# A dilated attention group in eight steps of two heads by four token tiles, with one copy-out place

## The chip, the cores and the metric

The kernel runs on one core of a Trainium2 chip. The metric is the time of one execution on the device, in microseconds (us). The engines are named as in the profile: PE is TensorE (PEld its weight loads), DVE is VectorE, ACT is ScalarE, POOL is GpSimd, SP is SyncE, which here only issues DMAs.

## The reference, cut to what matters

Two transformer blocks run one after the other over 1024 tokens of width 1024. The second block has, beside a latent attention, a dilated attention of 24 heads of width 64, in three groups of eight heads. The groups see keys at distances that are multiples of 1, 4 and 16, within a window:

```python
DIL_CONFIGS = ((128, 1), (512, 4), (2048, 16))
for g, (window, dilation) in enumerate(DIL_CONFIGS):
    o, lse = dilated_group(q[:, :, sl], k[:, :, sl], v[:, :, sl], dilation, window // (2 * dilation))
alpha = jax.nn.softmax(jnp.stack(lses, axis=0), axis=0)
out = jnp.sum(alpha[..., None] * outs, axis=0)
```

In `dilated_group` the scores of a query against its keys are masked, the maximum is subtracted, and out come exp, the sum `den`, and the weighted sum of the values. In the third group (dilation 16) the kernel puts the tokens of two residues into a tile of 128, so a tile of queries needs exactly one tile of 128 keys. In the first two groups it needs two (up to 256 keys).

## The kernel before

The dilated stage projects k, v and q of each group from the normalized input and runs the attention steps in the gaps. The work is written out by hand in slots. `D_UNITS` has 72 units (3 groups, then k, v, q, then 8 pieces each). Unit u is projected by PE in slots 2u and 2u + 1, in twelve matmuls of 512 columns each (`d_proj`, L1203). Slots 144 to 151 hold four units of the gates instead (units 16 to 19 of `gate_part`, L1118). After slot 151 comes the end of a phase, where PE, ACT and DVE wait for each other, and the gates go on with unit 20.

Each k or q unit is roped by DVE in slot 2u + 2: `rope_cos` (one instruction, L2279) and `rope_sin` (four instructions of 32 partitions, L2289, and an addition, L2295), which raises `roped`.

A step of attention takes one pair of heads (j) and some tiles of tokens. `step_at` says in which slot it begins. In that slot PE makes the scores (`d_scores`, L1219, into banks 3 and 4), DVE adds the mask and takes the maximum (`d_soft`, L2309), ACT takes the exponentials (`d_exp`, L1745). In the next slot PE transposes the result (`d_transposes`, L1232) and ACT copies it out of the accumulator (`d_pT`, L1754). In the slot after that PE multiplies by the values (`d_values`, L1251, bank 7), DVE copies the result into `osb` (`d_out`, L2318), and SP stores it (`d_store`, L628).

What decides about waits is the order within a slot, for each engine its own:

- PE: scores of a step that begins here, then twelve matmuls of the projection, then the values of the step two slots back, then the transposes of the step one slot back. Only the first two steps of a group have their scores behind the projection.
- DVE: `rope_cos`, `d_soft`, `d_out`, `rope_sin`. Only in the slot of a group's first step does `rope_sin` come before `d_soft`.
- ACT: `d_exp`, then `d_pT`.

The third group has 16 steps of two heads by two tiles, one in each of the slots 134 to 149. One step has 4 score matmuls of 128 columns, 4 of the mask and maximum, 4 exponentials, 4 transposes, 4 value matmuls, one copy of 512 and one of 256 elements, and 2 stores. A float32 matmul shows in the trace as two passes, so four of them are "x8". `osb` has two places of 256 elements, used in turn. The scores of a step wait for `d_max` of the step before, and the first of the steps of a head pair for `roped` of the pair's second q unit.

Of the kernel before, what the change touches and what calls it, by code (L numbers as in the profile page):

```python
# [98 lines left out]
def hybrid_blocks_kernel(nc, x, w_in, pool_w, pool_scale, attn_sinks, w_out, norm_pre, norm_post,  # L99
# [390 lines left out]
    def d_step(g, i):  # L490
        return 4 * 4 * g + i

    def step_of(g, i):

        j, r = divmod(i, 4)
        if g == 0:
            tiles = 2 * r, 2 * r + 1
        elif g == 1:
            tiles = 4 * (r % 2) + r // 2, 4 * (r % 2) + 2 + r // 2
        else:  # L500
            tiles = 2 * r, 2 * r + 1
        return j, tiles

    STEP_LAG = 4
    step_at = {}
    for u_, (g_, kind_, t_) in enumerate(D_UNITS):
        if kind_ == "q" and (g_ < 2 or t_ % 2):
            n_steps_ = 2 if g_ < 2 else 4
            for i_ in range(n_steps_):
                step_at[2 * u_ + STEP_LAG + i_] = g_, (2 * t_ if g_ < 2 else 4 * (t_ // 2)) + i_  # L510
    D_GATES = 4
# [13 lines left out]
    def gate_bank(u):  # L525

        return {47: 7, 19: 6, 20: 5}.get(u, u % 4)

# [42 lines left out]
    def _(sp):  # L571
# [51 lines left out]
        def d_store(g, i):  # L623
            n = d_step(g, i)
            j, tiles = step_of(g, i)
            sp.wait_ge(*after("d_out", n + 1))
            for b, t in enumerate(tiles):
                sp.dma_start(d_rows(g, t)[:, P * j:P * j + P].rearrange("p (a d) -> p a d", a=2),  # L628
                             osb[:, n % 2, 2 * b:2 * b + 2, :]).then_inc(sem(f"d_store{n % 2}"), 16)

        def stats_store(g):

            sp.wait_ge(*after("d_exp", G * d_step(g, 16)))
# [175 lines left out]
    def _(pe):  # L809
# [397 lines left out]
        def d_scores(g, i):  # L1207
            n = d_step(g, i)
            j, tiles = step_of(g, i)
            if i % (4 if g == 2 else 2) == 0:  # L1210
                q_unit = i // 2 if g < 2 else i // 2 + 1
                pe.wait_ge(*after("roped", 16 * g + 8 + q_unit + 1))
            if n >= 1:
                pe.wait_ge(*after("d_max", n))
            for b, t in enumerate(tiles):
                k0, nk, _, _ = window(g, t)
                for a in range(2):
                    rows = slice(HD * a, HD * a + HD)
                    m = pe.matmul(ps[:, 3 + a, 256 * b:256 * b + nk], qTd[rows, j % 2, P * t:P * t + P],  # L1219
                                  kTd[rows, j, k0:k0 + nk], start=True, stop=True)  # L1220
            m.then_inc(sem("d_scored"), 1)

        def d_transposes(g, i):
            n = d_step(g, i)
            pe.wait_ge(*after("d_exp", G * (n + 1)))
            if n >= 1:
                pe.wait_ge(*after("d_pT", n))
            c = 0
            for b, t in enumerate(step_of(g, i)[1]):
                for a in range(2):  # L1230
                    for c0, width, _, _, _ in window(g, t)[3]:
                        m = pe.transpose(ps[:, 5 + c // 4, (c % 4) * P:(c % 4) * P + P],  # L1232
                                         prd[n % 2][:, 2 * b + a, c0:c0 + width], ident[:])
                        c += 1
            m.then_inc(sem("d_T"), 1)
# [20 lines left out]
        for slot in range(D_SLOTS):  # L1256
# [3 lines left out]
            if slot < 2 * N_D:  # L1260
                d_proj(slot)
            else:
                u, part = divmod(slot - 2 * N_D, 2)
                if part == 0 and u < 3:
                    pe.wait_ge(*after("d_read", N_D - 2 + u))
                elif part == 0:
                    pe.wait_ge(*after("d_pT", 2 * 16))
                gate_part(16 + u, part)
# [8 lines left out]

        pe.wait_ge(*after("d_max", 2 * 3 * TT))
        pe.wait_ge(*after("d_pT", 2 * 3 * TT))

# [93 lines left out]
        for j in range(n_t + 5):  # L1374
            if j < n_t:
                m_scores(j)
            if j == 0:
                pe.wait_ge(*after("d_out", 2 * 3 * TT))
                gate_unit(47)
# [23 lines left out]
    def _(act):  # L1403
# [331 lines left out]
        def d_exp(g, i):  # L1735
# [5 lines left out]
            for b, t in enumerate(tiles):  # L1741
                nk = window(g, t)[1]
                for a in range(2):
                    h, o, p_ = 2 * j + a, dstat[:, g % 2, t, :], prd[n % 2][:, 2 * b + a, 0:nk]
                    act.activation(p_, p_, ACT.Exp, scale=-1.0, bias=o[:, h:h + 1], accum_out=o[:, H1 + h:H1 + h + 1]).then_inc(sem("d_exp"), 1)  # L1745

        def d_pT(g, i):
            n = d_step(g, i)
            act.wait_ge(*after("d_T", n + 1))
            if n >= 1:  # L1750
                act.wait_ge(*after("d_valued", n))
            nb = G if g == 2 else 2 * G
            src = ps[:, 5:7, :].rearrange("p b (j c) -> p (b j) c", c=P)
            act.activation(pTd[:, 0:nb, :], src[:, 0:nb, :], ACT.Copy).then_inc(sem("d_pT"), 1)  # L1754

        for slot in range(D_SLOTS):
# [12 lines left out]
            if slot == D_SLOTS - 2:  # L1769
                act.wait_ge(*after("d_scored", 2 * 3 * TT))  # L1770
                act.wait_ge(*after("stats_out", 48))
# [18 lines left out]
        act.wait_ge(*after("roped", 6 * TT))  # L1790
        act.wait_ge(*after("d_valued", 2 * 3 * TT))
        gate_evac(range(16, 16 + D_GATES), gt2)
# [160 lines left out]
    def _(dve):  # L1953
# [317 lines left out]
        def rope_cos(u, r, g, kind, t):  # L2271
# [4 lines left out]
            if kind == "q" and (g or j >= 2):  # L2276
                dve.wait_ge(*after("d_scored", d_step(g, 4 * (j - 2) + 4)))
            dve.wait_ge(*after("d_done", u + 1))
# [18 lines left out]
        def d_soft(g, i):  # L2297
# [7 lines left out]
            for b, t in enumerate(tiles):  # L2305
                nk, mc = window(g, t)[1:3]
                for a in range(2):
                    h = 2 * j + a
                    last = nc.vector.tensor_tensor_reduce(prd[n % 2][:, 2 * b + a, 0:nk], ps[:, 3 + a, 256 * b:256 * b + nk], masks[:, mc:mc + nk],  # L2309
                                                          -1.0, BIG, ALU.add, ALU.min, accum_out=dstat[:, g % 2, t, h:h + 1])  # L2310
            last.then_inc(sem("d_max"), 1)

        def d_out(g, i):
            n = d_step(g, i)
            dve.wait_ge(*after("d_valued", n + 1))
            if n >= 2:
                dve.wait_ge(*after(f"d_store{n % 2}", 32 * (n // 2)))
            nc.vector.tensor_copy(osb[:, n % 2].rearrange("p b d -> p (b d)"), ps[:, 7, 0:256]).then_inc(sem("d_out"), 1)  # L2318

        for slot in range(D_SLOTS):  # L2320
# [15 lines left out]
            if slot == D_SLOTS - 2:  # L2336
                group_stats = [stats[:, 0], stats[:, 1], dstat[:, 0]]
                nm = [x_[:, :, 0:H1] for x_ in group_stats]
                den = [x_[:, :, H1:] for x_ in group_stats]
                dve.wait_ge(*after("d_scored", 2 * 3 * TT))  # L2340
                dve.wait_ge(*after("d_exp", G * 2 * 3 * TT))
                dve.wait_ge(*after("stats_in", 32))
# [133 lines left out]
```

## Time and profile before

| | us |
|---|---|
| median of 3 timed runs | 1712.38 |
| the three | 1711.75, 1712.38, 1715.34 |
| profiled execution, its own time | 1715.64 |
| span of its trace | 1713.8 |
| PE busy | 1681.7 (98%) |
| DVE busy | 831.0 (48%) |
| ACT busy | 560.6 (33%) |

The own time lies 1.8 us above the span. A busy PE is a modelled figure, since its matmuls overlap; starts of instructions are the better measure.

### The profile page before, as it was taken

How to read it: one execution, taken by the hardware profiler on the slowest of the kernel's cores; microseconds unless marked ns; L12 is line 12 of the kernel's file. 1: busy time of each engine (PE TensorE's matmuls, PEld its weight loads, DVE VectorE, ACT ScalarE, POOL GpSimd, SP SyncE). 2: the span in 40 equal slices, each digit the busy share in tenths (PEclk: the TensorE clock that was granted, in tenths of full speed). 3: DMA queues.
4: the chain of work that ended last, by engine and by line, in shares of the span. 5: the costliest groups of instructions: out<-in, count | busy, mean ns of one | idle time of the engine just before them, and what ended most of it. 6: DMA issues, size and time to landing. Idle time of an engine off the chain costs nothing.

```text
span 1713.8 us, 22561 instructions
## 1 busy us (share of the span) xinstructions
PE 1681.7 (98%) x8729; PEld 1390.4 (81%) x8729; DVE 831.0 (48%) x1630; ACT 560.6 (33%) x1288; POOL 510.3 (30%) x400
## 2 busy tenths in 40 slices
PE   7999999999999999999999999999999999999998
PEld 6778778889878787888878887787787999988886
DVE  4430245344343614558076653645521888855724
ACT  5101456324333003440034200441113777741211
POOL 6124033023333333022211133015313745534310
PEclk9999999999999999999999999999999999999999
DMA  6113012233257232111320223117465635226322
GB/s 205 50 68 105 13 62 70 87 119 93 74 208 270 87 117 81 32 44 51 115 75 21 70 74 111 32 50 266 127 230 160 144 64 139 53 68 212 109 113 98
DMA packets 97130, 178.44 MB, mean 104 GB/s; under 512 B 13912, under 2 KB 33792, under 8 KB 96896
## 3 DMA queue, kind: packets, MB, share of 16 engines
q1 hardware_dynamic: 61120, 95.57, 19.2%
q10 hardware_dynamic: 35904, 81.44, 13.5%
q8 instruction: 69, 1.13, 0.3%
q14 instruction: 37, 0.30, 0.1%
HBM read 122.05 MB, written 54.92 MB: 103 GB/s over the span
## 4 chain that ended last, share of the span: by engine, by line
PE 92%; DVE 4%; issue 1%; DMA 1%; POOL 1%; ACT 1%; ACTq 0%; DVEq 0%; POOLq 0%
PE ps L1203 22%; PE ps L1118 14%; PE ps L824 13%; PE ps L1056 5%; PE ps L1370 5%; PE ps L1310 5%; PE ps L958 4%; PE ps L1251 4%; PE ps L1340 4%; PE ps L1323 3%; PE ps L879 3%; PE ps L1219 2%; PE ps L1232 2%; PE ps L1010 2%; DVE rope_swapped L2289 1%
## 5 line engine op out<-in xcount | busy, mean ns | idle before, releaser
L711 POOL TENSOR_SCALAR w_hi<-w_stage 128x1024 fp32r<-128x1024 f32 (+3 forms) x140 | 127.4, 917 | 995.8 <-PE ps L1203 366.8
L718 POOL TENSOR_TENSOR w_lo<-w_stage,w_hi 128x1024 fp32r<-128x1024 f32 (+3 forms) x140 | 271.8, 1949 | 8.9
L1203 PE MATMUL ps<-h2T_hi,w_hi 128*128 128x512 f32 x384 | 157.0, 409 | 0.7 <-ACT gate_tiles L1618 0.7
L1118 PE MATMUL ps<-h2T_hi,w_hi 128*128 128x512 f32 x384 | 153.4, 400 | 0.5 <-issue 0.3
L1203 PE MATMUL ps<-h2T_hi,w_lo 128*128 128x512 f32 x384 | 153.0, 398 | 0.0
L1118 PE MATMUL ps<-h2T_lo,w_hi 128*128 128x512 f32 x384 | 152.3, 397 | 0.0
L1203 PE MATMUL ps<-h2T_lo,w_hi 128*128 128x512 f32 x384 | 151.9, 396 | 0.0
L1118 PE MATMUL ps<-h2T_hi,w_lo 128*128 128x512 f32 x384 | 151.3, 394 | 0.0
L1745 ACT ACTIVATE probs_dil<-probs_dil,dil_stats_out 128x256 f32<-128x256 f32 (+2 forms) x192 | 87.6, 457 | 155.9 <-DVE dil_stats_out L2309 155.3
L2289 DVE SCALAR_TENSOR_TENSOR rope_swapped<-ps,sin_table_T 32x512 f32<-32x512 f32 x192 | 132.0, 687 | 3.5
L2404 DVE TENSOR_REDUCE small<-ps 128x1 f32<-128x1024 f32 x64 | 77.7, 1214 | 55.1 <-PE ps L1310 54.9
L1310 PE MATMUL ps<-k_mla,q_mla 128*128 128x512 f32 x384 | 104.0, 406 | 0.0
L743 POOL TENSOR_SCALAR p_mla<-p_mla,small 128x1024 f32<-128x1024 f32 x64 | 71.7, 1120 | 87.3 <-DVE small L2397 87.1
L1203 PEld LDWEIGHTS ps<-h2T_hi,w_hi 128*128 128x128 f32 x384 | 72.6, 189 | 27.0 <-issue 9.4
L1766 ACT ACTIVATE values_out<-ps 128x512 f32<-128x512 f32 x24 | 14.4, 598 | 231.2 <-PE ps L1203 231.2
L2279 DVE SCALAR_TENSOR_TENSOR qT_dil<-ps,cos_table_T 128x512 f32<-128x512 f32 x24 | 23.2, 965 | 137.3 <-PE ps L1203 137.3
L2391 DVE TENSOR_TENSOR pT_mla_lo<-ps,pT_mla_hi 128x512 fp32r<-128x512 f32 x128 | 81.9, 680 | 14.0 <-ACT pT_mla_hi L1853 14.0
L1118 PEld LDWEIGHTS ps<-h2T_hi,w_hi 128*128 128x128 f32 x384 | 72.1, 188 | 18.8 <-POOL w_lo L718 0.7
L1853 ACT ACTIVATE pT_mla_hi<-ps 128x512 fp32r<-128x512 f32 x128 | 69.7, 596 | 52.3 <-PE ps L1323 52.3
L1203 PEld LDWEIGHTS ps<-h2T_hi,w_lo 128*128 128x128 f32 x384 | 72.6, 189 | 17.5
L1118 PEld LDWEIGHTS ps<-h2T_hi,w_lo 128*128 128x128 f32 x384 | 72.1, 188 | 17.3
L1203 PEld LDWEIGHTS ps<-h2T_lo,w_hi 128*128 128x128 f32 x384 | 72.7, 189 | 16.2
(294 smaller groups left out, 3751.8 us busy)
## 6 DMA issues: line engine op xcount, KB each, us to landing
w_stage<-in_w_in SPq DMA_DIRECT2D x76, 512.0 KB, 3.9
w_stage<-in_w_out SPq DMA_DIRECT2D x16, 512.0 KB, 3.8
gate_scr<-gate_tiles ACTq DMA_DIRECT2D x16, 512.0 KB, 3.8
gates<-gate_scr ACTq DMA_DIRECT2D x32, 256.0 KB, 3.3
v_dil<-v_dil_scr SPq DMA_DIRECT2D x25, 256.0 KB, 3.3
v_dil_scr<-values_out SPq DMA_DIRECT2D x24, 256.0 KB, 2.0
dil_scr<-dil_out SPq DMA_DIRECT2D x96, 64.0 KB, 1.6
dil_nums<-dil_scr ACTq DMA_DIRECT2D x24, 256.0 KB, 4.1
```

Of the source, the lines that this page charges most:

```text
L711: last = nc.gpsimd.tensor_scalar(hi_, raw_, 1.0, 0.0, ALU.mult, ALU.add)
L718: last = nc.gpsimd.tensor_tensor(lo_, raw_, hi_.bitcast(F32), ALU.subtract)
L824: m = pe.matmul(acc, a, b, start=(i == 0 and j == 0), stop=(i == len(pairs) - 1 and j == 2))
L1056: m = pe.matmul(ps[:, Y_BANKS[t % 4] + half, :], a[:, k, tk], b[:, s, k, :], start=(k == 0 and j == 0), stop=(k == KT - 1 and j == 2))
L1118: m = pe.matmul(ps[:, gate_bank(u), :], a[:, s, k, P * m_:P * m_ + P], b[:, k, COLS * n:COLS * n + COLS], start=(k == 0 and j == 0), stop= ...
L1203: m = pe.matmul(bank, a, b, start=(k == 0 and i == 0), stop=(k == KT - 1 and i == 2))
L1310: m = pe.matmul(ps[:, 2 * (i % 2) + n, :], Q[:, a, q], K[:, b, COLS * n:COLS * n + COLS], start=(j == 0), stop=(j == 2))
L1370: m = pe.matmul(ps[:, u % 8, :], a, b, start=(k == 0 and j == 0), stop=(k == 3 and j == 2))
L1745: act.activation(p_, p_, ACT.Exp, scale=-1.0, bias=o[:, h:h + 1], accum_out=o[:, H1 + h:H1 + h + 1]).then_inc(sem("d_exp"), 1)
L2289: last = nc.vector.scalar_tensor_tensor(rot[out_rows, 0, :], ps[rows, d_bank(u), :], -HD ** -0.5 if kind == "q" else -1.0, sinT[rows, COLS ...
L2391: nc.vector.tensor_tensor(PTl[dst], ps[:, 4 + half, :].rearrange("p (j c) -> p j c", c=P), PTh[dst].bitcast(F32), ALU.subtract).then_inc(s ...
L2404: nc.vector.tensor_reduce(rstd[:, j % 8:j % 8 + 1], ps[:, 2 * (j % 2):2 * (j % 2) + 2, :].rearrange("p b c -> p (b c)"), AX_X, ALU.max, ne ...
```

## The change

The third group runs in 8 steps of two heads by four tiles. They begin in every other slot (134, 136, ..., 148). Each has 8 of all that a step had 4 of, one copy of 1024 elements and one of 512, and 4 stores. The scores take the places of 128 columns in banks 3 and 4, the transposes both banks 5 and 6. `osb` is one place for this group, so a copy-out waits for all the stores of the step before. Gate unit 19 goes from bank 6 to bank 3 and waits for the last `d_max`. The counts of steps and exponentials follow. The numbers of matmuls, masks, exponentials and stores over the whole group stay. With i < 2 the steps 0 and 1 still have their scores behind the projection; step 1 now begins in slot 136.

```diff
     def step_of(g, i):
+        if g == 2:
+            j, r = divmod(i, 2)
+            return j, tuple(range(4 * r, 4 * r + 4))
         j, r = divmod(i, 4)
...
+    def exps_of(n):
+        return G * n + G * max(n - 32, 0)
+    def place(g):
+        return P if g == 2 else 2 * P
+    def probs_of(g, n):
+        return prd[n % 2].rearrange("p j (x k) -> p (j x) k", k=place(g))
...
-            n_steps_ = 2 if g_ < 2 else 4
-            for i_ in range(n_steps_):
-                step_at[2 * u_ + STEP_LAG + i_] = g_, (2 * t_ if g_ < 2 else 4 * (t_ // 2)) + i_
+            for i_ in range(2):
+                step_at[2 * u_ + STEP_LAG + i_ * (1 if g_ < 2 else 2)] = g_, (2 * t_ if g_ < 2 else 2 * (t_ // 2)) + i_
...
-        return {47: 7, 19: 6, 20: 5}.get(u, u % 4)
+        return {47: 7, 20: 5}.get(u, u % 4)
...
-            if i % (4 if g == 2 else 2) == 0:
-                q_unit = i // 2 if g < 2 else i // 2 + 1
+            if i % 2 == 0:
+                q_unit = i // 2 if g < 2 else i + 1
                 pe.wait_ge(*after("roped", 16 * g + 8 + q_unit + 1))
...
-            pe.wait_ge(*after("d_exp", G * (n + 1)))
+            pe.wait_ge(*after("d_exp", exps_of(n + 1)))
...
-                    pe.wait_ge(*after("d_pT", 2 * 16))
+                    pe.wait_ge(*after("d_max", D_STEPS))
...
-            nb = G if g == 2 else 2 * G
-            src = ps[:, 5:7, :].rearrange("p b (j c) -> p (b j) c", c=P)
-            act.activation(pTd[:, 0:nb, :], src[:, 0:nb, :], ACT.Copy).then_inc(sem("d_pT"), 1)
+            act.activation(pTd[:], ps[:, 5:7, :].rearrange("p b (j c) -> p (b j) c", c=P), ACT.Copy).then_inc(sem("d_pT"), 1)
...
             dve.wait_ge(*after("d_valued", n + 1))
-            if n >= 2:
-                dve.wait_ge(*after(f"d_store{n % 2}", 32 * (n // 2)))
-            nc.vector.tensor_copy(osb[:, n % 2].rearrange("p b d -> p (b d)"), ps[:, 7, 0:256]).then_inc(sem("d_out"), 1)
+            for b in range(n % 2, n % 2 + 1) if g < 2 else range(2):
+                m = (n + 1 - b) // 2
+                if m:
+                    dve.wait_ge(*after(f"d_store{b}", 32 * m + 32 * max(m - 16, 0)))
+            dst = osb[:, n % 2].rearrange("p b d -> p (b d)") if g < 2 else osb[:].rearrange("p x b d -> p (x b d)")
+            nc.vector.tensor_copy(dst, ps[:, 7, 0:256 if g < 2 else 512]).then_inc(sem("d_out"), 1)
```

## Rows read from the trace of the kernel before

**Rows 1.** The page, part 1: busy time of each engine, share of the span.

```profile
PE 1681.7 (98%) x8729; PEld 1390.4 (81%) x8729; DVE 831.0 (48%) x1630; ACT 560.6 (33%) x1288; POOL 510.3 (30%) x400
```

**Rows 2.** The chain that ended last, 1060 to 1320: start, length, what.

```profile
1077.18 4.91 PE ps L1203 x12
...
1089.25 2.99 PE ps L1203 x12
...
1129.73 2.99 PE ps L1118 x12
...
1156.74 22.64 PE ps L1118 x96
```

**Rows 3.** The timeline at the third group's first steps: start, length, engine, line.

```profile
1068.15 0.71 PE L1219 MATMUL ps<-kT_dil,qT_dil 64*128 64x128 f32 x8
...
1072.24 0.29 DVE L2309 CUSTOM_DVE_ANT_0 probs_dil<-ps,masks 128x128 f32<-128x128 f32 x1
...
1073.09 0.08 DVE L2309 DVE_READ_ACCUMULATOR2_ANT dil_stats_out<- 128x1 f32 x1
1073.20 0.40 ACT L1745 ACTIVATE probs_dil<-probs_dil,dil_stats_out 128x128 f32<-128x128 f32 x1 [23.95 <-DVE dil_stats_out L2309]
...
1073.22 0.72 PE L1219 MATMUL ps<-kT_dil,qT_dil 64*128 64x128 f32 x8 [1.36 <-DVE dil_stats_out L2309]
...
1074.91 1.12 PE L1232 MATMUL ps<-ident,probs_dil 128*128 128x128 f32 x4 [0.97 <-ACT probs_dil L1745]
...
1076.51 0.57 ACT L1754 ACTIVATE probsT_dil<-ps 128x512 f32<-128x512 f32 x1
```

**Rows 4.** Windows of 20 us: length, busy by engine, PEclk, DMA share, GB/s.

```profile
220.00:240.00 20.00, 18.31 (x109) 14.79 (x106) 10.87 (x37) 10.47 (x31) 8.18 (x6) 0.91 0.21 63
1060.00:1080.00 20.00, 17.67 (x83) 13.46 (x82) 15.62 (x37) 5.42 (x25) 7.80 (x4) 0.86 0.29 94
1080.00:1100.00 20.00, 19.59 (x126) 16.19 (x125) 14.09 (x41) 6.39 (x26) 0.00 (x0) 0.97 0.09 23
```

**Rows 5.** The timeline of PE in the second group, one slot.

```profile
916.23 1.89 PE L1251 MATMUL ps<-v_dil,probsT_dil 128*128 128x64 f32 x16
917.95 1.04 PE L1232 MATMUL ps<-ident,probs_dil 128*128 128x128 f32 x8
918.93 1.14 PE L1219 MATMUL ps<-kT_dil,qT_dil 64*128 64x256 f32 x8
919.99 0.50 PE L1203 MATMUL ps<-h2T_hi,w_hi 128*128 128x512 f32 x1
```

**Rows 6.** The timeline of slots 142 to 144, third group.

```profile
1112.32 1.00 PE L1251 MATMUL ps<-v_dil,probsT_dil 128*128 128x64 f32 x8
...
1113.35 0.42 DVE L2318 COPY dil_out<-ps 128x256 f32<-128x256 f32 x1 [2.53 <-PE ps L1251]
...
1113.69 0.71 PE L1219 MATMUL ps<-kT_dil,qT_dil 64*128 64x128 f32 x8
...
1113.81 2.79 DVE L2289 SCALAR_TENSOR_TENSOR rope_swapped<-ps,sin_table_T 32x512 f32<-32x512 f32 x4
...
1114.34 0.50 PE L1203 MATMUL ps<-h2T_hi,w_hi 128*128 128x512 f32 x1
...
1116.70 1.12 DVE L2295 TENSOR_TENSOR qT_dil<-qT_dil,rope_swapped 128x512 f32<-128x512 f32 x1
...
1117.24 1.00 PE L1251 MATMUL ps<-v_dil,probsT_dil 128*128 128x64 f32 x8
...
1118.85 0.71 PE L1219 MATMUL ps<-kT_dil,qT_dil 64*128 64x128 f32 x8 [0.17 <-DVE dil_stats_out L2309]
```

**Rows 7.** The instructions of line 2228: duration ns min/median/max, first and last start.

```profile
L2228 DVE COPY cos_table_T<-ps x2: 680/686/692, 546.1 to 546.8; 128x512 f32<-128x512 f32 x2
```

**Rows 8.** Issues at line 628: duration ns min/median/max; then us to landing.

```profile
L628 SPq DMA_DIRECT2D dil_scr<-dil_out x96: 319/384/1540, 677.3 to 1157.3; - x96
...
DMA to landing us min/median/max: 1.5/1.6/3.7
```

More of the change, by code:

```diff
@@ L491, in d_step @@
         return 4 * 4 * g + i
+    D_STEPS = 2 * 16 + 8
     def step_of(g, i):
+        if g == 2:
+            j, r = divmod(i, 2)
+            return j, tuple(range(4 * r, 4 * r + 4))
         j, r = divmod(i, 4)
[L496 to L502, printed above, removed]
+        return j, (2 * r, 2 * r + 1) if g == 0 else (4 * (r % 2) + r // 2, 4 * (r % 2) + 2 + r // 2)
+    def exps_of(n):
[4 more added lines that the diff above has]
+        return prd[n % 2].rearrange("p j (x k) -> p (j x) k", k=place(g))
     STEP_LAG = 4
@@ L628, in d_store @@
                 sp.dma_start(d_rows(g, t)[:, P * j:P * j + P].rearrange("p (a d) -> p a d", a=2),
-                             osb[:, n % 2, 2 * b:2 * b + 2, :]).then_inc(sem(f"d_store{n % 2}"), 16)
+                             osb[:].rearrange("p x b d -> p (x b) d")[:, 2 * b + (n % 2 * G if g < 2 else 0):][:, 0:2, :]).then_inc(sem(f"d_store{n % 2}"), 16)
         def stats_store(g):
-            sp.wait_ge(*after("d_exp", G * d_step(g, 16)))
+            sp.wait_ge(*after("d_exp", exps_of(d_step(g, 16))))
             dst, src = st_d[g], dstat[:, g, :, :]
@@ L1218, in d_scores @@
                     rows = slice(HD * a, HD * a + HD)
-                    m = pe.matmul(ps[:, 3 + a, 256 * b:256 * b + nk], qTd[rows, j % 2, P * t:P * t + P],
+                    m = pe.matmul(ps[:, 3 + a, place(g) * b:place(g) * b + nk], qTd[rows, j % 2, P * t:P * t + P],
                                   kTd[rows, j, k0:k0 + nk], start=True, stop=True)
@@ L1232, in d_transposes @@
                         m = pe.transpose(ps[:, 5 + c // 4, (c % 4) * P:(c % 4) * P + P],
-                                         prd[n % 2][:, 2 * b + a, c0:c0 + width], ident[:])
+                                         probs_of(g, n)[:, 2 * b + a, c0:c0 + width], ident[:])
                         c += 1
@@ L1275, in _ @@
         phase_end(pe, "pe")
-        pe.wait_ge(*after("d_max", 2 * 3 * TT))
-        pe.wait_ge(*after("d_pT", 2 * 3 * TT))
+        pe.wait_ge(*after("d_max", D_STEPS))
+        pe.wait_ge(*after("d_pT", D_STEPS))
         def joint_transposes(u):
@@ L1377, in _ @@
             if j == 0:
-                pe.wait_ge(*after("d_out", 2 * 3 * TT))
+                pe.wait_ge(*after("d_out", D_STEPS))
                 gate_unit(47)
@@ L1743, in d_exp @@
                 for a in range(2):
-                    h, o, p_ = 2 * j + a, dstat[:, g % 2, t, :], prd[n % 2][:, 2 * b + a, 0:nk]
+                    h, o, p_ = 2 * j + a, dstat[:, g % 2, t, :], probs_of(g, n)[:, 2 * b + a, 0:nk]
                     act.activation(p_, p_, ACT.Exp, scale=-1.0, bias=o[:, h:h + 1], accum_out=o[:, H1 + h:H1 + h + 1]).then_inc(sem("d_exp"), 1)
@@ L1769, in _ @@
             if slot == D_SLOTS - 2:
-                act.wait_ge(*after("d_scored", 2 * 3 * TT))
+                act.wait_ge(*after("d_scored", D_STEPS))
                 act.wait_ge(*after("stats_out", 48))
@@ L1790, in _ @@
         act.wait_ge(*after("roped", 6 * TT))
-        act.wait_ge(*after("d_valued", 2 * 3 * TT))
+        act.wait_ge(*after("d_valued", D_STEPS))
         gate_evac(range(16, 16 + D_GATES), gt2)
@@ L2276, in rope_cos @@
             if kind == "q" and (g or j >= 2):
-                dve.wait_ge(*after("d_scored", d_step(g, 4 * (j - 2) + 4)))
+                dve.wait_ge(*after("d_scored", d_step(g, (4 if g < 2 else 2) * (j - 1))))
             dve.wait_ge(*after("d_done", u + 1))
@@ L2308, in d_soft @@
                     h = 2 * j + a
-                    last = nc.vector.tensor_tensor_reduce(prd[n % 2][:, 2 * b + a, 0:nk], ps[:, 3 + a, 256 * b:256 * b + nk], masks[:, mc:mc + nk],
+                    last = nc.vector.tensor_tensor_reduce(probs_of(g, n)[:, 2 * b + a, 0:nk], ps[:, 3 + a, place(g) * b:place(g) * b + nk], masks[:, mc:mc + nk],
                                                           -1.0, BIG, ALU.add, ALU.min, accum_out=dstat[:, g % 2, t, h:h + 1])
@@ L2339, in _ @@
                 den = [x_[:, :, H1:] for x_ in group_stats]
-                dve.wait_ge(*after("d_scored", 2 * 3 * TT))
-                dve.wait_ge(*after("d_exp", G * 2 * 3 * TT))
+                dve.wait_ge(*after("d_scored", D_STEPS))
+                dve.wait_ge(*after("d_exp", exps_of(D_STEPS)))
                 dve.wait_ge(*after("stats_in", 32))
```

## The prediction

> **What bounds the kernel now.** The page's first part comes first: PE is busy 98% of the span and DVE about half [rows 1]. So time moves only where PE starts its next instruction earlier or later. The chain that ended last says the same of the third group's steps [rows 2]: almost every piece is PE, and the projection pieces follow at a steady distance. From 1089.25 to 1129.73 there are four pairs of slots, 10.12 us each. The reader should see that this distance is not all PE work. The timeline of one slot [rows 6] shows PE waiting 0.17 us for DVE before the scores: `d_soft` comes behind `rope_sin` in DVE's queue.
>
> Then the timeline at the first steps [rows 3]. The scores of step 0 begin at 1068.15, but DVE is still roping, and `d_soft` begins only at 1072.24. PE waits 1.36 us before the scores of step 1 and 0.97 us before the transposes of step 0. After that comes a projection of 4.91 us [rows 2] where the others take 2.99. The windows show why [rows 4]: the granted clock averages 0.86 and 0.97 in the two windows there, so 0.14 x 20 + 0.03 x 20 = 3.4 us were lost to TensorE's lower level (1.2 instead of 2.4 GHz), 6.8 us at half speed. The only other window below 1.00 lost 0.09 x 20 = 1.8 us. So the start of the group is the delicate place: a wait there is paid twice.
>
> The sum is made against the profiled execution's own time, 1715.64, which lies 3.3 us above the median of 1712.38. The three timed runs show the same two values: 1715.34, and 1712.38 with 1711.75. A low stretch after the group's start that is there in some executions and absent in others fits this. Without it PE's chain would save about 3.0 of the 3.4 us (some of it lies on an idle PE), and 1715.6 - 3.0 = 1712.6. I take it that the median run is one without this stretch.
>
> **The steady part.** A pair of slots of the new kernel has scores, projection, values, projection, transposes. Starts on PE give each price: scores of the same number of columns 919.99 - 918.93 = 1.06 [rows 5], projection 1117.24 - 1114.34 = 2.90 [rows 6], values of sixteen passes 917.95 - 916.23 = 1.72 and transposes of eight 918.93 - 917.95 = 0.98 [rows 5]. The sum is 1.06 + 2.90 + 1.72 + 2.90 + 0.98 = 9.56 us, 0.56 less than 10.12. That is the gain, if nothing makes PE wait: fewer changes between kinds of work, and the DVE wait gone.
>
> **The new wait for `roped`.** The change takes nothing from DVE but half of its copies' fixed cost: a copy of 512 elements takes 0.69 [rows 7], two of 256 take 0.84 [rows 6]. What moves is when `d_out` can run. It waits for the values, and `rope_sin` stands behind it. Counted from the start of the scores in an even slot, the values begin at 1.06 + 2.90 = 3.96, end 1.89 later [rows 5] at 5.85, the copy begins 0.03 later (1113.35 against 1113.32 [rows 6]) and ends at 6.57, and the rope's sine part takes 1116.70 + 1.12 - 1113.81 = 4.01 [rows 6]. `roped` comes at 10.6. The scores of the next even slot are due at 9.56, and those of steps 2, 4 and 6 need just this `roped`, of the second q unit of their pair of heads. So PE waits 1.0 to 1.1 us three times. For the odd steps the lateness reaches `d_soft` only, whose end then comes near 4.0; eight exponentials end at 7.3, before the transposes at 8.6. What is queued behind the waiting scores on PE is everything, a projection first. The wait could be 0, were the sine part sooner by 1.1, so the bounds for the three are 0 and 3.3; the queue order speaks for 3.2.
>
> **The start.** Until 1068.15 nothing changes. The scores of step 0 take 1.06, the projection of slot 135 ends at 1068.15 + 1.06 + 2.90 = 1072.1. `d_soft` starts at 1072.24 as before, since it waits for the rope, not for the scores. Four take 1073.09 + 0.08 - 1072.24 = 0.93 [rows 3], eight about 1.8: 1074.0. The eight exponentials before ran from 1073.20 to 1076.51, 3.3 us [rows 3]. So the transposes begin at 1077.4, and PE has nothing to do for 5.3 us: step 1's scores, which filled part of this, now stand behind the projection of slot 136. I am confident that this drops the clock, since 1.36 and 0.97 us did it before. The low stretches cost 1.8 and 3.4 us [rows 4]; PE is dense from its return on, so I take 2.2, near the smaller, with bounds 0 and 3.4.
>
> The Trainium skill, "TensorE: Matmul & The Clock Gate", section "What's actually happening", says that the lower level is the default and that activity releases it, and that the number of slow matmuls varies from run to run of one kernel. By that rule a timed run of the kernel before can miss the low stretch that its profile shows, and the one after cannot; the three times of before agree, and no row here shows it directly.
>
> **The sum, as a running clock of the scores' starts.** Step 1: 1077.4 + 0.98 + 2.90 + 2.2 = 1083.5. Step 2 waits for `roped` behind step 1's own chain: 1.06 + 1.89 + 0.03 + 0.69 + 4.01 + 0.05 = 7.7, so 1091.2 (its values follow the scores at once). Step 3: +9.56, 1100.8. Step 4: +10.6, 1111.4. Step 5: 1121.0. Step 6: 1131.6. Step 7: 1141.2. Then scores, projection, values, projection, transposes (9.56), and projection 2.90, values 1.72, projection 2.8 and 0.3 to the next phase: 17.3, so gate unit 20 begins at 1158.5. Before it began at 1156.74 [rows 2]. The change costs 1.7 us against the profiled execution (1717.3). Against a median run without the low stretch it costs 1.7 + 3.0 = 4.7: 1712.4 + 4.7 = 1717.1, say 1717.
>
> **Costed at nothing.** The stores: four issues of 0.38 and a landing of 1.6 [rows 8] are 3.1 us after the copy, and the next copy comes 9.6 after; without that cover each us too many would be PE's by way of `rope_sin`. The copy of 1024 on ACT has the projection of the next slot as cover. Gate unit 19 waits for the last `d_max`, some 7 us before it in DVE's queue. After the phase everything hangs on PE's end as before: ACT's evacuations wait for the last `d_out` and the coefficients, which come some 2 us before PE's end, as they did.
>
> The Trainium skill, "Perfetto Trace Analysis", section "Identifying Performance Opportunities", says that the same gap repeated can mean too few buffers. It speaks against the single copy-out place; by the row of the stores the slack is over 5 us, so by the rule a repeated gap would have to show at the copies, and I give that a small chance.
>
> **Rivals.**
> - *The low stretch belongs to the median run of before too*, and the 3.3 us between profile and median are something else. Then 1712.4 + 1.7 = 1714.1, no measurable change. For it: only four times are known. 0.25.
> - *Faster.* DVE isn't late for `roped` and the start costs no more than before: what is left is 0.56 for each of eight steps, 1712.4 - 4.5 = 1707.9. It decides if the sine part ends by 9.5 us instead of 10.6 and the first exponentials overlap the masks. Against it: both queues are in order, and `d_exp` waits for the last of eight. 0.10.
> - *More low stretches*: the waits of 1.1 us drop the clock as well, 1.8 us [rows 4] for one more, 1719. Against it: they stand alone between dense stretches. 0.10.
> - *The single place binds.* With the longest issue and landing [rows 8], 4 x 1.54 + 3.7 = 9.9 us, a copy would wait about 1 us seven times: 1724. 0.03.
>
> **How the numbers follow.** My forecast has 0.52: 1717. Its own range, from the bounds, is 1715 to 1718.5 (low clock between 1 and 3.4). The 8-in-10 range takes in the first rival and one more low stretch: 1712.5 to 1719.5. What a measurement of this kernel can tell is about 0.2%, 3.4 us. Of my forecast three quarters lie above that (0.39), of the first rival a little (0.04), of the last two all (0.13): slower 0.56, faster 0.10, no difference 0.34.
>
> **What would show it.** In the profile after: PE idle for about 5 us before the first transposes of the group, ended by ACT; a stretch of low clock right behind it; scores of steps 2, 4 and 6 waiting about 1 us for L2295 (`roped`), not for L2309; odd to even steps 10.6 apart, even to odd 9.6. If the idle time is under 3 us, the reading of the start is wrong; if the three waits are missing, that of the queue. The median comes out otherwise if the low clock in timed runs isn't that of the profile.

## The result, and the profile after

The changed kernel takes 1715.68 us (median of 12 runs, 1713.6 to 1716.7) against 1713.14 (12 runs, 1710.0 to 1718.22) of the kernel before: ratio 1.0017, 95% interval 1.0009 to 1.0024. By this ratio it is slower by 2.9 us (2.5 between the medians), and the interval, 1.5 to 4.1 us, leaves out zero; but it is still within the 0.2% that the prediction counts as no difference. The profiled execution has 1716.7 as its own time and a span of 1714.9, before 1715.64 and 1713.8.

The page's first part answers to [rows 1]. As many matmuls, nearly the same busy share:

```profile
PE 1679.2 (98%) x8729; PEld 1389.6 (81%) x8729; DVE 834.1 (49%) x1622; ACT 559.5 (33%) x1280; POOL 512.1 (30%) x400
```

The chain that ended last, third group, answers to [rows 2] (start, length, what). The line numbers have moved: scores L1228, transposes L1241, values L1260, projection L1212, gate units L1127, masks L2316, exponentials L1754, the rope's sine part L2296 and L2302, copies out L2328.

```profile
1076.37 1.97 PE ps L1241 x8
1078.34 4.48 PE ps L1212 x12
1082.81 1.09 PE ps L1228 x16
...
1090.63 1.16 PE ps L1228 x16
...
1100.23 1.09 PE ps L1228 x16
...
1110.84 1.16 PE ps L1228 x16
...
1120.44 1.09 PE ps L1228 x16
...
1131.06 1.16 PE ps L1228 x16
...
1140.67 1.09 PE ps L1228 x16
...
1157.85 22.64 PE ps L1127 x96
```

The reader is to see two distances between the starts of scores: 9.6 us from an even step to an odd one (1090.63 to 1100.23, 1110.84 to 1120.44) and 10.6 from an odd one to an even one (1100.23 to 1110.84, 1120.44 to 1131.06). Before, a pair of slots took 10.12 throughout.

The waits of PE from 1055 to 1165 (total us, times, longest):

```profile
PE ps L1241 <- ACT probs_dil L1754: 5.0, 2, 4.7
PE ps L1228 <- DVE qT_dil L2302: 2.7, 3, 1.1
```

The timeline at the first step answers to [rows 3]:

```profile
1067.55 1.16 PE L1228 MATMUL ps<-kT_dil,qT_dil 64*128 64x128 f32 x16
...
1070.11 1.17 DVE L2302 TENSOR_TENSOR qT_dil<-qT_dil,rope_swapped 128x512 f32<-128x512 f32 x1
...
1071.32 0.29 DVE L2316 CUSTOM_DVE_ANT_0 probs_dil<-ps,masks 128x128 f32<-128x128 f32 x1
...
1076.37 1.97 PE L1241 MATMUL ps<-ident,probs_dil 128*128 128x128 f32 x8 [4.66 <-ACT probs_dil L1754]
...
1082.74 1.16 PE L1228 MATMUL ps<-kT_dil,qT_dil 64*128 64x128 f32 x16
```

The windows of 20 us (the column behind the counts is the granted clock) answer to [rows 4]:

```profile
1060.00:1080.00 20.00, 15.34 (x74) 12.21 (x73) 13.66 (x29) 4.21 (x17) 7.81 (x4) 0.88 0.26 81
1080.00:1100.00 20.00, 19.15 (x125) 15.78 (x123) 12.54 (x44) 7.40 (x33) 0.00 (x0) 0.95 0.10 27
```

PE idles once, 4.66 us, before the first transposes, with TensorE's lower level behind it: the eight transposes take 1.97 us where eight took 1.04 at 2.4 GHz [rows 5].

A yardstick is used in all that follows: **the distance** from the start of step 0's scores to that of gate unit 20, the whole third group. It was 1156.74 - 1068.15 = 88.59 before and is 1157.85 - 1067.55 = 90.30 after. It has three parts that can be told apart in a timeline: from step 0's scores to the first transposes (8.82 in the changed kernel, 1067.55 to 1076.37), from there to step 1's scores (6.37, to 1082.74), where a low clock shows, and from there to gate unit 20 (75.11). The medians carry other differences between executions as well.

### The profile page after: what moved, and what is told of

The parts are those of the page before. It is cut to its first block, busy times and chain, and to the rows that moved or that the text cites. A ratio compares the mean times of both kernels' runs of the same rounds, so it can differ in the third digit from the quotient of the medians.

```text
span 1714.9 us, 22505 instructions
## 1 busy us (share of the span) xinstructions
PE 1679.2 (98%) x8729; PEld 1389.6 (81%) x8729; DVE 834.1 (49%) x1622; ACT 559.5 (33%) x1280; POOL 512.1 (30%) x400
## 4 chain that ended last, share of the span: by engine, by line
PE 94%; DVE 4%; ACT 1%; issue 1%; DMA 0%; POOL 0%; DVEq 0%; POOLq 0%
PE ps L1212 22%; PE ps L1127 14%; PE ps L833 14%; PE ps L1065 5%; PE ps L1379 5%; PE ps L1319 5%; PE ps L1260 4%; PE ps L967 4%; PE ps L1349 4%; PE ps L1332 3%; PE ps L888 3%; PE ps L1228 2%; PE ps L1241 2%; PE ps L1019 2%; DVE rope_swapped L2296 1%; PE ps L992 1%
## 5 line engine op out<-in xcount | busy, mean ns | idle before, releaser
L1212 PE MATMUL ps<-h2T_hi,w_hi 128*128 128x512 f32 x384 | 157.1, 409 | 0.7 <-ACT gate_tiles L1627 0.7
L1127 PE MATMUL ps<-h2T_hi,w_hi 128*128 128x512 f32 x384 | 154.3, 402 | 0.3 <-issue 0.3
L1212 PE MATMUL ps<-h2T_hi,w_lo 128*128 128x512 f32 x384 | 152.7, 398 | 0.0
L1212 PE MATMUL ps<-h2T_lo,w_hi 128*128 128x512 f32 x384 | 151.8, 395 | 0.0
L1127 PE MATMUL ps<-h2T_hi,w_lo 128*128 128x512 f32 x384 | 151.6, 395 | 0.0
L1127 PE MATMUL ps<-h2T_lo,w_hi 128*128 128x512 f32 x384 | 151.2, 394 | 0.0
L1754 ACT ACTIVATE probs_dil<-probs_dil,dil_stats_out 128x256 f32<-128x256 f32 (+2 forms) x192 | 87.4, 456 | 151.9 <-DVE dil_stats_out L2316 151.7
L2296 DVE SCALAR_TENSOR_TENSOR rope_swapped<-ps,sin_table_T 32x512 f32<-32x512 f32 x192 | 132.0, 687 | 3.5
L1212 PEld LDWEIGHTS ps<-h2T_hi,w_hi 128*128 128x128 f32 x384 | 72.6, 189 | 26.2 <-issue 9.2
L1212 PEld LDWEIGHTS ps<-h2T_hi,w_lo 128*128 128x128 f32 x384 | 72.6, 189 | 17.7
L1127 PEld LDWEIGHTS ps<-h2T_hi,w_lo 128*128 128x128 f32 x384 | 72.1, 188 | 18.1
L1127 PEld LDWEIGHTS ps<-h2T_hi,w_hi 128*128 128x128 f32 x384 | 72.1, 188 | 17.3 <-issue 0.7
L1212 PEld LDWEIGHTS ps<-h2T_lo,w_hi 128*128 128x128 f32 x384 | 72.6, 189 | 15.9
```

The costliest lines, as they stand in the source:

```text
L1127: m = pe.matmul(ps[:, gate_bank(u), :], a[:, s, k, P * m_:P * m_ + P], b[:, k, COLS * n:COLS * n + COLS], start=(k == 0 and j == 0), stop= ...
L1212: m = pe.matmul(bank, a, b, start=(k == 0 and i == 0), stop=(k == KT - 1 and i == 2))
L2296: last = nc.vector.scalar_tensor_tensor(rot[out_rows, 0, :], ps[rows, d_bank(u), :], -HD ** -0.5 if kind == "q" else -1.0, sinT[rows, COLS ...
```

## The experiments

**The order in DVE's queue, in the steady part.** In the third group `rope_sin` goes ahead of `d_out`.

```diff
-            if slot - 2 in step_at:
+            late = slot - 2 in step_at and step_at[slot - 2][0] == 2
+            if slot - 2 in step_at and not late:
                 d_out(*step_at[slot - 2])
...
                 rope_sin(*done)
+            if late:
+                d_out(*step_at[slot - 2])
```

> The changed kernel with one edit: in the third group's slots DVE does rope_sin before d_out instead of after it. Theory (roped is late because the copy-out stands before it in DVE's queue and waits for the values): the three waits of PE before the scores of steps 2, 4 and 6 (0.53, 1.06 and 1.07 us in the profile after) are gone, pairs odd to even go from 10.7 to 9.6 us, and the distance from step 0's scores to gate unit 20 falls by 2.7 us, from 90.3 to 87.6. The wait of about 5 us at the start and the low clock behind it stay. Rival (DVE is simply short of time in these slots, so any order is late): the waits only move to another instruction and the distance falls by less than 1 us. Rival (the late copy-out then holds up the values or the stores): a new wait on bank 7 shows at L1260 and the gain is below 1 us.

The three waits for `roped` are gone. PE's waits from 1055 to 1165:

```profile
PE ps L1241 <- ACT probs_dil L1754: 5.2, 2, 4.9
PE ps L1127 <- issue: 0.3, 1, 0.3
```

The same place in the changed kernel (first fence) and in this one (second), timelines:

```profile
1104.16 1.89 PE L1260 MATMUL ps<-v_dil,probsT_dil 128*128 128x64 f32 x16
...
1106.09 0.69 DVE L2328 COPY dil_out<-ps 128x512 f32<-128x512 f32 x1 [1.93 <-PE ps L1260]
1106.81 2.79 DVE L2296 SCALAR_TENSOR_TENSOR rope_swapped<-ps,sin_table_T 32x512 f32<-32x512 f32 x4
...
1109.70 1.08 DVE L2302 TENSOR_TENSOR qT_dil<-qT_dil,rope_swapped 128x512 f32<-128x512 f32 x1
1110.84 1.16 PE L1228 MATMUL ps<-kT_dil,qT_dil 64*128 64x128 f32 x16 [1.06 <-DVE qT_dil L2302]
```

```profile
1101.49 2.79 DVE L2296 SCALAR_TENSOR_TENSOR rope_swapped<-ps,sin_table_T 32x512 f32<-32x512 f32 x4
...
1104.38 1.18 DVE L2302 TENSOR_TENSOR qT_dil<-qT_dil,rope_swapped 128x512 f32<-128x512 f32 x1
1105.59 0.69 DVE L2328 COPY dil_out<-ps 128x512 f32<-128x512 f32 x1
```

In the first, DVE stands 1.93 us at the copy, which waits for the values, and the rope is stuck behind it; in the second it ropes in that time. The distance is 86.57, 3.7 less. From step 1's scores to gate unit 20 it is 72.25 in place of 75.11, 2.9 less, of which 2.7 are the waits; the other 0.9 are a cheaper start, since here the two windows have a clock of 0.91 and 1.00 in place of 0.88 and 0.95. The time is 1714.48 (11 runs; ratio 1.0008, 0.9999 to 1.0016), only 1.2 under the changed kernel where 2.7 were expected. The granted clock of whole executions differs too: five of the eleven have a mean of 0.995 or 0.996, none of the changed kernel's twelve has. At the same mean clock the gain is there, though on few runs: at 0.998 the medians are 1712.7 (3 runs) and 1715.6 (7), at 0.997 1713.2 (3) and 1716.0 (5). Why these executions have more low clock stays open.

**The order at the first step.** In the third group `d_soft` goes ahead of `rope_sin` at the first step.

```diff
-            first = slot in step_at and step_at[slot][1] == 0
+            first = slot in step_at and step_at[slot][1] == 0 and step_at[slot][0] < 2
```

> The changed kernel with one edit: in the slot of the third group's first step DVE masks the scores before rope_sin, as in its other steps. Theory (PE's wait at the start is the chain of a late mask, eight masks and eight exponentials): the masks begin about 1.1 us after the scores' start instead of 3.8, and PE's wait before the first transposes falls from 4.7 us to about 2.2. The low clock may or may not follow a wait of 2.2 us; if it does the distance from step 0's scores to gate unit 20 falls by 2.5 us from 90.3, if not by about 4.6. Rival (the wait is made by ACT or by the exponentials alone): it stays over 4 us.

The line to read is again the wait of the transposes (the second below), now 2.1 at the longest; the three for `roped` stay. In this profile no low stretch follows, as the window shows; the timeline has the transposes and step 1's scores:

```profile
PE ps L1228 <- DVE qT_dil L2302: 2.7, 3, 1.1
PE ps L1241 <- ACT probs_dil L1754: 2.4, 2, 2.1
```

```profile
1060.00:1080.00 20.00, 17.89 (x110) 14.26 (x109) 15.27 (x44) 4.22 (x17) 7.78 (x4) 1.00 0.21 65
```

```profile
1073.38 1.09 PE L1241 MATMUL ps<-ident,probs_dil 128*128 128x128 f32 x8 [2.11 <-ACT probs_dil L1754]
...
1077.20 1.16 PE L1228 MATMUL ps<-kT_dil,qT_dil 64*128 64x128 f32 x16
```

The distance is 85.21, 5.1 less than 90.30: half of it idle time (4.66 - 2.11 = 2.55), half low clock. The second number can be had directly: from the first transposes to step 1's scores the changed kernel takes 1082.74 - 1076.37 = 6.37 us, this one 1077.20 - 1073.38 = 3.82, again 2.55 less. The time is 1713.22 (12 runs; 1.0007, 0.9996 to 1.0018). Of the twelve, 4 have a mean granted clock of 0.999, with a median of 1711.6, and 8 at most 0.998, median 1713.9. This fits a wait of 2.1 us that has low clock behind it in some executions only, but a mean over the execution doesn't show where its low clock lies.

**The single copy-out place.** A second place is taken from a scratch buffer (`ts`), so that each copy waits only for the stores of two steps before.

```diff
+    def out_place(g, n):
+        if g < 2:
+            return osb[:, n % 2].rearrange("p b d -> p (b d)")
+        return osb[:].rearrange("p x b d -> p (x b d)") if n % 2 else ts[:]
...
+            nc.vector.tensor_copy(out_place(g, n), ps[:, 7, 0:256 if g < 2 else 512]).then_inc(sem("d_out"), 1)
```

> The changed kernel with a second copy-out place for the third group (the tile that held the values on their way out serves the even steps), so a copy-out waits for the stores of two steps back. Theory (the stores are over 5 us before the next copy): same in all distances to 0.1 us, and the same time within its interval. Rival (the single place binds): the waits of PE before the scores of steps 2, 4 and 6 shrink and the time falls by 1 us or more.

The waits do not move (total, times, longest):

```profile
PE ps L1246 <- ACT probs_dil L1759: 5.2, 2, 4.9
PE ps L1233 <- DVE qT_dil L2307: 2.7, 3, 1.1
```

The distance is 90.02, 0.3 less and so outside the 0.1 that I had allowed, but the difference lies ahead of the group's first copy: from step 1's scores to gate unit 20 it is 75.12, before 75.11. The time is 1716.35 (10 runs; 1.0019, 1.001 to 1.0029). The single place costs nothing that shows.

**The kernel before with the mask first.** The line of the second experiment, in the kernel before.

> The kernel before with the same edit as in the second run: masks before rope_sin in the slot of the third group's first step. Theory (in the profiled execution of before, waits of 1.36 and 0.97 us brought a low stretch that cost 3.4 us; in most timed executions there is none): both waits are gone or below 0.5 us and no low stretch shows in the profile at the group's start. The median falls by 2 to 2.5 us against before if timed runs mostly lack the low stretch, and by 4.5 to 6 us if they mostly have it. Its spread is narrower than that of before (8 us over 12 runs), if the low stretch made that spread.

The distance falls from 88.59 to 86.61, but the waits did not go as I expected: one of 1.8 us is left, and the scores of step 2 have it. The timeline shows the cause, the mask of step 1 behind the rope of the next unit:

```profile
1069.59 2.79 DVE L2289 SCALAR_TENSOR_TENSOR rope_swapped<-ps,sin_table_T 32x512 f32<-32x512 f32 x4
...
1072.49 1.08 DVE L2295 TENSOR_TENSOR qT_dil<-qT_dil,rope_swapped 128x512 f32<-128x512 f32 x1
1073.60 0.29 DVE L2309 CUSTOM_DVE_ANT_0 probs_dil<-ps,masks 128x128 f32<-128x128 f32 x1
...
1074.59 0.92 PE L1219 MATMUL ps<-kT_dil,qT_dil 64*128 64x128 f32 x8 [1.78 <-DVE dil_stats_out L2309]
```

A low stretch is there too:

```profile
1060.00:1080.00 20.00, 18.22 (x90) 14.03 (x90) 15.68 (x37) 5.33 (x25) 7.80 (x4) 0.91 0.27 87
```

The time is 1712.07 (11 runs; 0.9999, 0.999 to 1.0008): no difference, where I had expected a fall of 2 us at the least.

**Both orders, in the changed kernel.** The two edits together.

> The changed kernel with both edits: rope_sin before d_out in the third group, and masks before rope_sin in its first step's slot. Theory (two separate causes): the distance from step 0's scores to gate unit 20 is 85.1 us (as with the second edit alone and no low stretch) less 2.7 = 82.5, or 84 with a low stretch. The median falls by about 4 against the changed kernel's 1715.7, to about 1711. Rival (the two share one cause and don't add): the distance is 84 to 85 without a low stretch.

83.88, the branch with a low stretch, which is there in the window: the same wait of 2.1 us as in the second experiment, this time with a clock of 0.91 (there 1.00).

```profile
1060.00:1080.00 20.00, 17.89 (x96) 13.90 (x94) 13.47 (x29) 4.21 (x17) 7.77 (x4) 0.91 0.24 73
```

The time is 1709.62 (8 runs), ratio 0.9977, 0.9966 to 0.9987: the first version whose interval lies below the kernel before.

**Both orders, in the kernel before.** This asks what the large steps are worth by themselves.

> The kernel before with the same two edits, to see what the larger steps are worth when neither order hurts. With masks first alone, a wait of 1.8 us stayed (scores of step 2 wait for the masks of step 1, which stand behind rope_sin) and the odd slots' wait of 0.2 us too. Theory: the wait of 1.8 us stays, since the copy isn't its cause; the waits of the odd slots (0.24 us a pair) go, since rope_sin no longer waits for the values: distance 86.6 less about 1.2 = 85.4 with a low stretch, 84 without. So small steps stay 1.5 us or more behind the large ones of the fifth run. Rival (the large steps have no merit of their own): equal or better than it.

The distance is 83.64 without a low stretch; the fifth experiment's 83.88 has 1.55 of low clock in it (from the transposes to step 1's scores 5.37 there, 3.82 in the second experiment), so like for like the large steps lead by 1.3. The wait of 1.8 us stays, this time at full clock:

```profile
1075.82 0.72 PE L1219 MATMUL ps<-kT_dil,qT_dil 64*128 64x128 f32 x8 [1.78 <-DVE dil_stats_out L2309]
```

```profile
1060.00:1080.00 20.00, 18.22 (x99) 14.20 (x97) 18.38 (x42) 5.33 (x25) 7.82 (x4) 1.00 0.35 114
```

What counts is its steady part, the values of successive slots in the chain:

```profile
1084.45 0.84 PE ps L1251 x8
...
1089.37 0.84 PE ps L1251 x8
...
1094.29 0.84 PE ps L1251 x8
```

4.92 us per slot are 9.84 per pair, against 9.54 to 9.55 of the changed kernel with both orders. So the large steps save 0.3 us per pair and not 0.56; the rest of the 0.56 was the mask's wait, which small steps lose as well once the order is mended. The time is 1711.23 (12 runs; 0.999, 0.9981 to 0.9999), 1.6 above the fifth experiment's, though the two intervals overlap.

**The start filled with work.** The fifth experiment's kernel, and step 0's transposes go behind the projection of slot 136.

```diff
+            if slot - 2 in step_at and step_at[slot - 2] == (2, 0):
+                d_transposes(2, 0)
             if first:
                 d_scores(*step_at[slot])
...
-            if slot - 1 in step_at:
+            if slot - 1 in step_at and step_at[slot - 1] != (2, 0):
                 d_transposes(*step_at[slot - 1])
```

> The changed kernel with both edits, and the transposes of the group's first step moved behind the projection of slot 136 and ahead of step 1's scores. Theory (PE's wait at the start is only an order that leaves it nothing to do): PE waits at most 0.6 us at one place, no low stretch at the start, distance from step 0's scores to gate unit 20 80.1 us against 90.3 of the changed kernel and 88.6 of the profiled one before. Median 1707 to 1708.5, faster than both. Rival (the wait only moves, to the values of step 0, which wait for the copy of 1024): a wait over 1 us at L1260.

The distance is 80.01. PE's waits, the window of the start, then the chain in the steady part:

```profile
PE ps L1127 <- issue: 0.3, 1, 0.3
PE ps L1241 <- ACT probs_dil L1756: 0.2, 1, 0.2
```

```profile
1060.00:1080.00 20.00, 19.93 (x120) 16.32 (x119) 17.82 (x48) 6.11 (x27) 7.81 (x4) 1.00 0.25 79
```

```profile
1082.44 1.09 PE ps L1228 x16
...
1091.99 1.09 PE ps L1228 x16
...
1147.34 22.64 PE ps L1127 x96
```

The time is 1707.75 (5 runs, 1706.17 to 1708.25), ratio 0.9961, 0.9949 to 0.9973. It beats both kernels: 5.3 us under the one before in its own comparison and 7.9 under the changed one's median.

**Step 1's scores ahead of the projection.** The prediction put part of the start's cost on their new place; here PE does them first.

```diff
-            first = slot in step_at and step_at[slot][1] < 2
+            first = slot in step_at and step_at[slot][1] < (2 if step_at[slot][0] < 2 else 1)
```

> The changed kernel with one edit: the scores of the third group's second step stand ahead of the projection of slot 136, not behind it. The prediction named their place behind it as what leaves PE without work. Theory (in PE's queue they come behind step 0's transposes either way, and roped for step 2 hangs on step 0's values, which keep their place): PE's wait of 4.7 us stays, the wait of 0.5 us for roped before step 2 grows to about 1.05 as at steps 4 and 6 and takes up what the earlier scores give; distance from step 0's scores to gate unit 20 90.3 to within 0.3. Rival (their place matters): distance lower by 1 us or more.

The distance is 89.09 and the time 1717.48 (8 runs; 1.0027, 1.0017 to 1.0037). The distance fell by 1.2, and so by as much as I had set for the rival. But the wait for ACT is still 4.5 and the three for `roped` are 3.2 together, as the theory had it. What fell is the low clock: the two windows from 1060 to 1100 have 1.00 and 0.91 (0.09 x 20 = 1.8 us lost) in place of 0.88 and 0.95 (3.4), and 0.5 of this goes to the longer wait before step 2. No gain shows in the time. So the place of these scores does not make the long wait; in PE's queue they come behind the transposes either way.

**The wait filled with matmuls that nobody reads.** The changed kernel with 18 extra matmuls into bank 7, whose content is spent by then, ahead of the first transposes.

```diff
+            if slot - 1 in step_at and step_at[slot - 1] == (2, 0):
+                pe.wait_ge(*after("d_out", 32))
+                for _ in range(18):
+                    pe.matmul(ps[:, 7, :], wh[:, index["q2"] % 2, 0, 0:P], h2h[:, 0, 0:COLS], start=True, stop=True)
```

> The changed kernel with 18 extra matmuls of 512 columns into bank 7, which nobody reads, in PE's wait before the first transposes of the third group; no other work is left out or moved. They take 18 x 0.233 = 4.2 of the 4.7 us. Theory (the low stretch behind the wait is a cost of its own, about 2 us): no low stretch shows there, the transposes begin when they did, and the distance from step 0's scores to gate unit 20 falls by 1.5 to 2 us from 90.3, though PE does more work. The median falls by as much from 1715.7. Rival (the low clock comes from elsewhere, or hides nothing): distance within 0.5 us of 90.3 or longer.

```profile
1069.78 1.16 PE L1228 MATMUL ps<-kT_dil,qT_dil 64*128 64x128 f32 x16
...
1079.21 1.09 PE L1241 MATMUL ps<-ident,probs_dil 128*128 128x128 f32 x8 [1.07 <-ACT probs_dil L1758]
...
1083.03 1.16 PE L1228 MATMUL ps<-kT_dil,qT_dil 64*128 64x128 f32 x16
```

```profile
1060.00:1080.00 20.00, 18.93 (x96) 14.90 (x95) 16.23 (x30) 3.19 (x16) 7.79 (x4) 1.00 0.36 121
1080.00:1100.00 20.00, 19.15 (x128) 15.83 (x127) 12.25 (x44) 8.43 (x34) 0.00 (x0) 1.00 0.09 24
```

The real work waits longer than before: the transposes begin 9.43 us after step 0's scores, in the changed kernel 8.82. Yet the distance is 88.36, 1.94 less, since from the transposes to step 1's scores it is 3.82 in place of 6.37. The time is 1713.15 (12 runs; 0.9998, 0.9988 to 1.0007), 2.5 less than the changed kernel. This shows the low clock as a cost apart from the wait: 2.55 us.

**The same in the kernel before.** 5 and 4 extra matmuls in its two waits at the start. If the low stretch belonged to all its executions, the median would fall by the whole 3.0.

> The kernel before with extra matmuls of 512 columns into bank 7, which nobody reads, in PE's two waits at the third group's start: 5 ahead of step 1's scores (1.17 of 1.36 us), 4 ahead of step 0's transposes (0.93 of 0.97). No work is left out or moved. Theory (the low stretch there is an event of some executions and costs 3.0 us of PE's chain when it comes): no low stretch at the group's start in the profile, distance from step 0's scores to gate unit 20 85.6 against 88.6. If about half of the timed executions of before have the stretch, the mean falls by about 1.5 us and the median by 0.5 to 1.5; if hardly any has it, by less than 0.5; if nearly all, by 2.5 to 3.

The distance is 85.60, 3.0 less than 88.59, with the window at 1.00:

```profile
1060.00:1080.00 20.00, 19.91 (x101) 15.27 (x100) 16.48 (x38) 5.37 (x25) 7.81 (x4) 1.00 0.35 116
```

The time is 1711.62 (11 runs, ratio 0.9997, 0.9987 to 1.0007) against 1712.5 beside it: 0.9 less, and not 3.0. So a part of the executions of before never had the stretch. How large a part, this run does not tell: the median speaks for about half by what I had expected, the mean, which fell by 0.25 only (1712.34 against 1712.59), for hardly any, and the interval allows anything from 2.2 us less to 1.2 more.

## Why the prediction was right, and where it was off

**The running clock held.** In the prediction's own classes the result is "no difference", to which it gave 0.34, and not "slower", to which it gave 0.56; the time lies in the range of its own forecast, 1715 to 1718.5. The profile it foretold much more closely than the time. The prediction's times of the scores' starts less 0.6, by which step 0 itself lay earlier in this execution, against the profile: 1082.9 and 1082.8, 1090.6 and 1090.6, 1100.2 and 1100.2, 1110.8 and 1110.8, 1120.4 and 1120.4, 1131.0 and 1131.1, 1140.6 and 1140.7, gate unit 20 at 1157.9 and 1157.85. The distance grew by 90.30 - 88.59 = 1.71 us where 1.7 was predicted.

- *The steady pair*, predicted 9.56: 9.60 in the changed kernel, 9.54 in the fifth experiment. The prediction gave two sources of the 0.56, fewer changes between kinds of work and the DVE wait gone, and did not divide it. The sixth experiment does: 0.3 belong to the large steps, and the rest is a wait that an order in the kernel before would have cured too.
- *The wait for `roped`*, predicted three times 1.0 to 1.1: 2.7 in all, of which the two steady ones are up to 1.1 each and the one before step 2 the rest, about 0.5. Its cause is the order in DVE's queue; this is shown by the first experiment, in which it goes with the order alone.
- *The idle start*, predicted 5.3: 4.66. I had the masks begin at the old time; in the profile they began 0.9 earlier (1071.32 against 1072.24), of which 0.6 is step 0 itself. Mask behind rope makes more than half of it, shown by the second experiment (2.1 in place of 4.7); the rest is the chain of eight masks and eight exponentials behind the scores. That step 1's scores had left this place, as the prediction has it, is no cause: moved ahead of the projection they left the wait at 4.5 (eighth experiment).
- *The low clock*, predicted 2.2, bounds 0 and 3.4: 2.55, from the two pieces above. Counted from step 0's scores, the transposes came 0.43 sooner than computed (8.82 against 9.25) and the low clock cost 0.35 more, so the two misses at the start nearly cancel; that is luck. The prediction calls the window 220 to 240 the only other one below 1.00, which is a misreading: from 1700 to the end of the span the trace of before is at 0.84. But it is at 1.00 up to 1705 and PE has no work after 1710, so the sum does not hang on it.
- *Stores, copies, gate unit 19 at nothing*: right; no wait names them, and the third experiment finds nothing to win there.

**The term that was mis-sized** is the last one, "I take it that the median run is one without this stretch", worth 3.0 us. For an execution without the stretch the sum was right: the tenth experiment's distance is 85.60 and the changed kernel's 90.30, 4.70 apart as forecast, and the medians are 1711.62 and 1715.68, 4.1 apart (3.4 by the two ratios). But the median of before is 1713.14 over 12 runs, 0.8 above the 1712.38 of three.

The 78 executions of the kernel before that were made beside the experiments tell more. 34 of them have a mean granted clock of 0.999 or more, with a median of 1711.46; the other 44 have 0.998 or less and a median of 1714.0. All 12 executions of the changed kernel have 0.997 or 0.998. The profiles show what such a mean stands for. Apart from the end of the span, those of the second, sixth and seventh experiment have no low window and 0.999; those with one window at 0.91, wherever it lies, have 0.998 (first, fifth, tenth) or 0.999 (ninth); the five with more low clock than that have 0.996 or 0.997. So the two groups are not executions with and without the stretch at the group's start: in the seventh experiment PE waits for nothing there, and four of its five executions have 0.998. A sign of the start is the lowest part of the scale. Of the 78, 27 have 0.997 or less; of the 28 executions of the three kernels in which the start is filled (seventh, ninth, tenth) none has. By this, which is an argument and not a measurement of the timed executions, about a third of before's have the stretch at the start beside another one, and more may have it alone.

So the median of before lies between the kinds of execution, and what was measured is a mixture. Against the upper group the changed kernel is 1715.68 - 1714.0 = 1.7 us slower, against the lower one 4.2; that these are near the 1.7 and the 4.7 of the prediction shows nothing by itself, since the groups are cut by all low clock and not by the start's. The rival whose whole difference was 1.7 (1714.1) was as near the truth as my 1717: they lie 1.6 below and 1.3 above.

The Trainium skill, "TensorE: Matmul & The Clock Gate", section "What's actually happening", calls the number of slow matmuls variable between runs of one kernel; it says so of the start of a kernel, and the prediction carried it over to a stretch in the middle. What was measured there agrees with that: a wait of 2.1 us had a clock of 1.00 behind it in one kernel's profile and 0.91 in the other's, and the clocks of the 78 lie between 0.996 and 1.000. What the rule could not give was the share of executions, and there I chose all or nothing.

The Trainium skill, "Perfetto Trace Analysis", section "Identifying Performance Opportunities", reads a repeated gap as a possible lack of buffers. Here the repeated gap was 1.06 us before the scores; a second place left it as it was (1.1), a changed order removed it. In this case the trace speaks for the order, not the buffer.

**What the change did, then.** It saved 0.56 us in each steady pair, and gave it back in three waits that DVE's order made and a long one at the start, which the low clock made dearer. None belongs to the large steps as such: with orders to suit them and the start filled, the same steps are 5.3 us faster than the kernel before. Not all of that is theirs either. Small steps with both orders are 1.8 us faster than before, and filling their start as well was not tried; as an estimate, their distance of 83.64 less the one wait of 1.8 is 81.8, still 1.8 behind the 80.01 of large steps.

## What to carry to other kernels

When steps are made larger, the work that used to fall between them stands in other places of every queue: go through each in-order queue and ask what waits behind the first instruction that now waits longer, since moving it can be free (here 2.7 us of waits for a few lines). Look first at the start of a stage, where a wait can be paid a second time in TensorE's clock, and fill it with a later projection or even with matmuls that nobody reads. And before a forecast leans on three timed runs, ask whether the kernel has executions of several kinds, because then a median is a mixture; the mean granted clock beside each time tells, but not where the low clock lies.

## What the runs showed of the hardware

- After waits near 2 us the lower clock level came or did not: 2.1 us had 1.00 (second experiment) or 0.91 (fifth) in the window of 20 us, 1.8 us had 0.91 (fourth) or 1.00 (sixth). The profiles don't show what decides. Waits of 4.5 to 4.9 us had a low stretch behind them in all four profiles (the changed kernel and the first, third and eighth experiments), the separate ones of up to 1.1 us, before the scores of steps 2, 4 and 6, in none.
- Low stretches also turn up with no connection to the group: the window 220 to 240 is at 0.91 to 0.93 in six of the twelve profiles (before, after, third, fourth, eighth and ninth experiment) and at 1.00 in the other six, and the tenth experiment has one at 0.91 from 660 to 680. I can't say what sets them off.
- Extra matmuls made a kernel faster: 18 of them, 4.37 us of useless work, took 1.94 us off the distance and 2.5 us off the median. In the kernel before, nine of them took 3.0 us off the distance, and no change of the time that is clear of its noise.
